# Receptance and key projections of the second block: three weight chunks as seven half-block products each

## The reference

```python
x = rmsnorm(x, final_norm_g)            # end of the first block
xx = _token_shift(x) - x
xr, xk = x + xx * mu[0], x + xx * mu[2]     # xw, xa, xg, xv likewise, with their own mu
r = xr @ w_r                            # 512 x 1024 by 1024 x 1024
k = xk @ w_k                            # the same size
w, a, g: small products xw @ w1, xa @ a1 (64 columns each), xg @ g1 (128 columns)
v = xv @ w_v
kk = k * k_k; its norm over each head of 64 features is taken here too
```

## Time and profile before

| | us |
|---|---|
| median of three runs | 2712.99 |
| lowest and highest run | 2707.52 and 2714.55 |
| profiled execution, its own time | 2716.39 |
| profiled execution, span of the trace | 2714.6 |
| this stage, from its first product to the start of the last `gemm` | 1081.34 to 1222.62 |

### The profile page before, as it was taken

The page is one execution under the profiler, slowest core; times in us unless marked ns, Lnnn a source line. Parts: engine busy times, 40 slices in busy tenths (PEclk is TensorE's granted clock), DMA queues, the critical chain, the costliest instruction groups (busy, mean ns, idle before and its releaser), DMA issues. The chain is left out here.

```text
span 2714.6 us, 46714 instructions
## 1 busy us (share of the span) xinstructions
PE 2584.1 (95%) x20608; PEld 1977.9 (73%) x20608; DVE 1243.7 (46%) x1965; ACT 515.3 (19%) x1032; POOL 548.9 (20%) x361
## 2 busy tenths in 40 slices
PE   6999889989999999999899999999999999999998
PEld 4555568854888887444788568888878764888886
DVE  2213235454899944222677454442242474545233
ACT  3222122321111101112455210000010261000001
POOL 0000055520000000000222023443333100443342
PEclk9999999999999999999999999999999999999999
DMA  7123100021212123111000021222222101122220
GB/s 300 71 116 155 63 2 3 3 94 62 93 67 89 66 85 128 47 62 63 34 4 4 2 93 67 89 93 93 90 83 93 63 1 62 63 93 93 77 78 32
DMA packets 17369, 195.32 MB, mean 72 GB/s; under 512 B 1896, under 2 KB 3048, under 8 KB 5392
## 3 DMA queue, kind: packets, MB, share of 16 engines
q1 hardware_dynamic: 17168, 192.34, 18.8%
HBM read 190.22 MB, written 2.12 MB: 71 GB/s over the span
## 5 line engine op out<-in xcount | busy, mean ns | idle before, releaser
L3322 PE MATMUL psum<-arena,weight_ring 128*128 128x256 f32 x3072 | 671.2, 379 | 2.9 <-ACT arena L3212 2.9
L3322 PEld LDWEIGHTS psum<-arena,weight_ring 128*128 128x128 f32 x3072 | 582.7, 190 | 86.0 <-ACT arena L3212 5.3
L1862 PE MATMUL psum<-arena,weight_ring 128*128 128x256 f32 x1584 | 348.2, 381 | 5.0 <-DVE arena L2038 4.0
L1862 PEld LDWEIGHTS psum<-arena,weight_ring 128*128 128x128 f32 x1584 | 301.6, 191 | 48.7 <-issue 6.4
L492 PE MATMUL psum<-arena,weight_ring 128*128 128x512 f32 (+1 forms) x672 | 250.5, 531 | 3.4 <-DMA weight_ring<-in_w_in 2.6
L492 PEld LDWEIGHTS psum<-arena,weight_ring 128*128 128x128 f32 x672 | 127.5, 193 | 118.5 <-issue 102.6
L2408 POOL TENSOR_TENSOR arena<-arena,consts_sb 128x512 f32<-128x512 f32 x9 | 11.4, 1271 | 726.8 <-ACT arena L2784 688.8
L3421 POOL TENSOR_TENSOR weight_ring<-arena,weight_ring 128x1024 f32<-128x1024 f32 x32 | 79.3, 2477 | 378.3 <-PE psum L3322 378.3
L229 PE MATMUL psum<-arena,weight_ring 128*128 128x512 f32 x320 | 137.8, 592 | 0.0
L3411 POOL TENSOR_TENSOR arena<-weight_ring 128x1024 f32<-128x1024 f32 x32 | 77.1, 2408 | 288.5 <-issue 172.7
L3444 ACT ACTIVATE arena<-psum 128x512 f32<-128x512 f32 (+1 forms) x24 | 12.6, 524 | 621.0 <-PE psum L3322 621.0
(11 more groups left out here) (482 smaller groups left out, 3688.8 us busy)
## 6 DMA issues: line engine op xcount, KB each, us to landing
weight_ring<-in_mlp_up SPq DMA_DIRECT2D x16, 2048.0 KB, 8.0
weight_ring<-in_mlp_down SPq DMA_DIRECT2D x16, 2048.0 KB, 8.0
weight_ring<-in_ada SPq DMA_DIRECT2D x12, 2048.0 KB, 11.4
weight_ring<-in_gate_up SPq DMA_DIRECT2D x11, 2048.0 KB, 7.8
weight_ring<-in_w_in SPq DMA_DIRECT2D x7, 2048.0 KB, 11.6
weight_ring<-in_w_o SPq DMA_DIRECT2D x4, 2048.0 KB, 7.9
weight_ring<-in_w_kv SPq DMA_DIRECT2D x4, 2048.0 KB, 8.0
weight_ring<-in_down_a SPq DMA_DIRECT2D x4, 1536.0 KB, 6.1
```

The source lines that it names most:

```text
L1862: mm = pe.matmul(g.banks[i][:, pair * half:(pair + 1) * half], left[:, j, pair * P:(pair + 1) * P], right(j), start=first and j == 0, stop ...
L3322: mm = pe.matmul(g.banks[i][:, pair * HALF:(pair + 1) * HALF], left[:, j, pair * P:(pair + 1) * P], right(j), start=first and j == 0, stop ...
```

## The change

Chunk 0 of `w_r` stays as it is. Chunks 1, 2 and 3 (the second of `w_r`, both of `w_k`) are multiplied by seven products of half blocks into banks 0 to 6. `key_sums` moves from bank 6 to bank 7 and to later places: its first half behind the two 64-column products, its second half behind the third small product. POOL gets a block of its own, with four weight sums a chunk; the first pair, `weight_sums(1)`, has nothing to wait for but the landed chunk. DVE gets `sides` (four input sums for each of two inputs) and `take` (seven additions a chunk); ACT gets one copy a chunk and loses twelve, and its squares move behind the last `take`. Five semaphores are added.

```diff
@@ -2168,10 +2168,27 @@
+    near, far = slice(0, HALF), slice(HALF, SEQ)
+    side = [view(g, V_AT + 1024 * n, 4, HALF) for n in range(4)]
+    s1 = view(g, 20480, 4, 256)
+    p1, u2, v_ = (view(g, 21504 + 512 * n, 2, HALF) for n in range(3))
...
-        s = stage_sems(g, ctx, "lora_in", "xx", "first", "mixed", "ksq", "kstat", "kroot", "kinv", *RMS_SEMS)
+        s = stage_sems(g, ctx, "lora_in", "xx", "first", "mixed", "ksq", "kstat", "kroot", "kinv", "w_sums", "side", "prod", "p1",
+                       "took", *RMS_SEMS)
...
+        def out_part(c, half, toks):
+            first = 4 * (c % 2) + 2 * half
+            return outs[c // 2][:, first:first + 2, (near, far)[toks]]
...
@@ -2187,7 +2204,7 @@
-                            mm = pe.matmul(g.banks[6][:, 8 * p + 2 * tile:8 * p + 2 * tile + 2],
+                            mm = pe.matmul(g.banks[7][:, 8 * p + 2 * tile:8 * p + 2 * tile + 2],
...
@@ -2208,15 +2225,54 @@
+                def product(c, i, left, right):
+                    if c == 1:
+                        if i != 1:
+                            pe.wait_ge(g.acc_free, group0 + 4)
+                    elif i == 0:
+                        pe.wait_ge(s.p1, c - 1)
+                    elif i == 6:
+                        pe.wait_ge(g.acc_free, group0 + 4 * c)
+                    else:
+                        pe.wait_ge(s.took, 6 * (c - 2) + (0, 1, 3, 5, 2, 6)[i])
+                    for pair in (0, 1):
+                        cols = slice(pair * P, (pair + 1) * P)
+                        for j in range(4):
+                            mm = pe.matmul(g.banks[i][:, pair * HALF:(pair + 1) * HALF], left[:, j, cols], right[:, j, :],
+                                           start=j == 0, stop=j == 3)
+                    if i < 6:
+                        mm.then_inc(s.prod, 1)
+                    else:
+                        mm.then_inc(g.acc_ready, 4)
...
                 rms_pe(g, pe, s, norm)
                 first_receptances()
-                group = group0 + 4
-                for j in range(2):
-                    pe.wait_ge(s.mixed, KD * (j + 1))
-                    for i in (0, 1) if j else (1,):
-                        group = gemm(g, pe, chunk0 + 2 * j + i, group, KD, 512,
-                                     [(0, lambda k: mixed[j % 2][:, k, :], SEQ)])
-                key_sums(0)
+                for c in (1, 2, 3):
+                    source = mixed[c // 2]
+                    sides = 4 * (c // 2)
+                    a11, a12, a21, a22 = quads(c)
+                    landed(pe, c)
+                    pe.wait_ge(s.mixed, KD * (c // 2 + 1))
+                    if c == 1:
+                        product(c, 1, a12, source[:, 4:8, near])
+                        product(c, 0, a11, source[:, 0:4, near])
+                    else:
+                        product(c, 0, a11, source[:, 0:4, near])
+                        product(c, 1, a12, source[:, 4:8, near])
+                    pe.wait_ge(s.w_sums, 4 * c - 3)
+                    pe.wait_ge(s.side, sides + 1)
+                    product(c, 2, s1, side[0])
+                    pe.wait_ge(s.w_sums, 4 * c - 2)
+                    pe.wait_ge(s.side, sides + 2)
+                    product(c, 3, a21, side[2])
+                    pe.wait_ge(s.w_sums, 4 * c - 1)
+                    pe.wait_ge(s.side, sides + 3)
+                    product(c, 4, a11, side[1])
+                    pe.wait_ge(s.side, sides + 4)
+                    product(c, 5, a22, side[3])
+                    pe.wait_ge(s.w_sums, 4 * c)
+                    product(c, 6, a12, source[:, 4:8, far])
+                group = group0 + 16
                 w = chunk_at(g, pe, chunk0 + 4, KD, 256)
                 for j, (lo, hi, row) in enumerate(((0, 64, 0), (64, 128, 64), (128, 256, 0))):
                     pe.wait_ge(s.mixed, KD * (j + 3))
@@ -2228,28 +2284,49 @@
                     mm.then_inc(g.acc_ready, 1)
                     group += 1
                     if j == 1:
-                        key_sums(4)
+                        key_sums(0)
+                key_sums(4)
                 pe.wait_ge(s.mixed, KD * 6)
                 gemm(g, pe, chunk0 + 5, group, KD, 512, [(0, lambda k: values[k], SEQ)])
...
+            @block.gpsimd
+            def _(pool):
+                def weight_sums(c):
+                    a11, a12, a21, a22 = quads(c)
+                    landed(pool, c)
+                    if c >= 2:
+                        pool.wait_ge(s.prod, 6 * (c - 2) + 3)
+                    pool.tensor_tensor(s1, a21, a22, ALU.add).then_inc(s.w_sums, 1)
+                    pool.wait_ge(s.w_sums, 4 * c - 3)
+                    pool.tensor_tensor(a21, a11, a21, ALU.subtract).then_inc(s.w_sums, 1)
+
+                def second_sum(c):
+                    a11, a12, a21, a22 = quads(c)
+                    pool.wait_ge(s.w_sums, 4 * c - 2)
+                    pool.wait_ge(s.prod, 6 * (c - 1) + 2)
+                    pool.tensor_tensor(a11, s1, a11, ALU.subtract).then_inc(s.w_sums, 1)
+
+                def fourth_sum(c):
+                    a11, a12, a21, a22 = quads(c)
+                    pool.wait_ge(s.w_sums, 4 * c - 1)
+                    pool.tensor_tensor(a12, a12, a11, ALU.subtract).then_inc(s.w_sums, 1)
+
+                weight_sums(1)
+                for c in (1, 2, 3):
+                    second_sum(c)
+                    fourth_sum(c)
+                    if c < 3:
+                        weight_sums(c + 1)
...
+                def lora_out(i):
...
-                        act.activation(kn, g.banks[6][:, 0:64], ACT.Sqrt).then_inc(s.kroot, 1)
+                        act.activation(kn, g.banks[7][:, 0:64], ACT.Sqrt).then_inc(s.kroot, 1)
+                    if i >= 19:
                         ins = act.activation(outs[2][:, i - 19, :], bank[:, :], ACT.Copy)
                     elif i == 16:
                         ins = act.activation(wa[0:64, :], bank[0:64, :], ACT.Tanh)
...
-                    if 8 <= i < 16:
-                        act.wait_ge(g.acc_free, group0 + i + 1)
-                        if i == 15:
-                            act.wait_ge(s.kstat, 1)
-                        act.activation(ksq[:, (i - 8) % 7, :], outs[1][:, i - 8, :], ACT.Square,
-                                       scale=g.v.k_k[:, i - 8:i - 7]).then_inc(s.ksq, 1)
+
...
+                for i in range(4):
+                    act.wait_ge(g.acc_ready, group0 + i + 1)
+                    act.activation(outs[0][:, i, :], g.banks[2 * ((group0 + i) % 3)][:, :], ACT.Copy).then_inc(g.acc_free, 1)
+                for c in (1, 2, 3):
+                    act.wait_ge(s.prod, 6 * (c - 1) + (2 if c == 1 else 1))
+                    if c >= 2:
+                        act.wait_ge(s.took, 6 * (c - 2) + 2)
+                    act.activation(p1.rearrange("p a n -> p (a n)"), g.banks[0][:, :], ACT.Copy).then_inc(s.p1, 1)
+                act.wait_ge(g.acc_free, group0 + 16)
+                for p in range(KD):
+                    if p == 7:
+                        act.wait_ge(s.kstat, 1)
+                    act.activation(ksq[:, p % 7, :], outs[1][:, p, :], ACT.Square, scale=g.v.k_k[:, p:p + 1]).then_inc(s.ksq, 1)
+                    if p < 2:
+                        lora_out(16 + p)
+                for i in range(18, 23):
+                    lora_out(i)
                 act.wait_ge(g.acc_free, group0 + 23)
 
...
+                def sides(j):
+                    source = mixed[j]
+                    x11, x12, x21, x22 = source[:, 0:4, near], source[:, 0:4, far], source[:, 4:8, near], source[:, 4:8, far]
+                    dve.wait_ge(s.mixed, KD * (j + 1))
+                    if j == 1:
+                        dve.wait_ge(g.acc_ready, group0 + 8)
+                    dve.tensor_tensor(side[0], x12, x11, ALU.subtract).then_inc(s.side, 1)
+                    dve.tensor_tensor(side[2], x22, x12, ALU.subtract).then_inc(s.side, 1)
+                    dve.wait_ge(s.side, 4 * j + 1)
+                    dve.tensor_tensor(side[1], x22, side[0], ALU.subtract).then_inc(s.side, 1)
+                    dve.wait_ge(s.side, 4 * j + 3)
+                    dve.tensor_tensor(side[3], x21, side[1], ALU.subtract).then_inc(s.side, 1)
+
+                def add(out, bank, other):
+                    both = g.banks[bank][:, :].rearrange("p (a n) -> p a n", a=2)
+                    return dve.tensor_tensor(out, both, other, ALU.add)
+
+                def take(c):
+                    done, took = 6 * (c - 1), 6 * (c - 1)
+                    if c >= 2:
+                        dve.wait_ge(s.took, took)
+                        dve.wait_ge(g.acc_free, group0 + 4 * c)
+                    dve.wait_ge(s.p1, c)
+                    dve.wait_ge(s.prod, done + 2)
+                    add(out_part(c, 0, 0), 1, p1).then_inc(s.took, 1)
+                    dve.wait_ge(s.prod, done + 5)
+                    add(u2, 4, p1).then_inc(s.took, 1)
```

(38 more changed lines are left out.)

14 lines of the change are left out of this document (11 added, 3 removed).

## The result

The changed kernel takes 2697.52 us in the median of 4 runs (2695.71 to 2697.79) against 2712.32 beside it (4 runs, 2707.52 to 2714.55): a ratio of 0.9941 with a 95% interval of 0.9925 to 0.9957, so 14.8 us less, where 7.9 were forecast. The forecast of 2705.1 with its range of 2700.0 to 2710.5 is missed on the low side. The profiled execution took 2697.26 us; before, it was 2716.39.

A forecast was written before the change was run, and what follows sets the result against it. PE's own work was taken to bound the stage; -9.89 products, +1.05 seam, +0.9 start and 0 clock gave -7.9 us, so 2705.1 us from the median 2712.99, range 2700 to 2710.5.

The forecast's parts named there:

- Products: Chunks 1 to 3 of the changed stage: 72.52 us in place of 82.41, so 9.89 us removed.
- All the slacks: In those chunks POOL, DVE, ACT and transfers finish before PE needs them; the tightest POOL sum has 4.4 us.
- The seam: Behind chunk 3 PE's first small product waits for the last addition of `take(3)`: 1.05 us added.
- The start, the port: At the stage's start a POOL sum holds up DVE's line 2284 through the shared port: 0.9 us added.
- The clock, "0 net": Half clock behind the two `key_sums` still costs 5.1 us, as before, so nothing is gained or lost.
- or also at the start: Half of a rival: 3.4 us at half clock at the stage's start, +1.7 us; chance 0.20 with the other half.
- `mix(2)` beside POOL's sums: Rival: POOL's sums delay DVE's `mix(2)` by up to 9.6 us; slower only if `take(2)` is late; chance 0.04.
- -9.89 + 1.05 + 0.9 + 0 = -7.9 us: The changed stage's products, seam, start and clock summed, and taken as the whole kernel's gain.
- POOL's clears, costed at 0: Five more POOL clears at the stage's exit, 0.07 us each on POOL alone, add 0 to the kernel.

The follow-up runs named there:

- Experiment 4: Two edits, each alone, to the changed kernel: POOL's first weight sum waits for the eighth mix, 2692.96 us; key sums dealt out one at a time, 2692.67 us.
- before_place47: The kernel before with exactly 47 more TensorE instructions (already satisfied waits) ahead of the last chunk's products of the changed stage: 2704.82 us, ratio 0.9980.
- before_again: The kernel before, unchanged, run once more: 2713.13 us, ratio 0.9999.
- after_again: The changed kernel, unaltered, run once more: 2698.26 us, ratio 0.9949.
- place 128: The kernel before with 128 more TensorE instructions ahead of the last chunk of the changed stage (place: added instructions modulo 256): 2709.72 us, ratio 0.9997.

## Why the prediction was wrong, step by step

- **Products: right.** 72.52 us were forecast for the three chunks and 72.69 measured, with no idle note. All the slacks held.
- **The seam: right.** 1.05 forecast; 0.94 idle, released by the last addition.
- **The start, the port: right.** "1.6 us" for line 2284 was 1.54, and the wait ahead of the first product grew by 0.85 for 0.9 forecast.
- **The clock, "0 net": mis-sized by 1.7 us.** Behind the sums the half clock stayed at 10.2 us, but behind the wait of 2.27 us at the start stand 3.4 more. That was half of a rival ("or also at the start"), priced at +1.7 and given 0.20 together with its other half. Experiment 4 shows that it comes with the POOL sums and goes with them. With this term the sum is -7.9 + 1.7 = -6.2, and the stage gave -6.1.
- **`mix(2)` beside POOL's sums: the mechanism came, and the cover held**, as its rival said it would have to fail for a loss.
- **The step that failed** is the one that carried the sum of one stage over to the kernel: "-9.89 + 1.05 + 0.9 + 0 = -7.9 us". It holds no term for the stages behind the change but POOL's clears, costed at 0. So it put the unchanged mixing stage at nothing, and that stage gave as much as the changed one. The 303 instructions that the change adds were costed as PE time alone; that they move all that follows against the instruction packets was in no term and no rival. That is worth 5.4 us by before_place47's ratio (0.0020 x 2710.65; 2.4 to 8.4 by its interval). In the two profiled executions the stage gave 6.2: the stalls fell by 6.1, half clock cost 1.7 more, and 1.8 less is unexplained. The repeats, before_again and after_again, give 6.3: 4.1 of stalls, 1.7 of half clock and 0.5.
- **What stays open.** 6.1 and some 6 make 12, of 14.8 measured. That is inside the interval of the result (11.7 to 20.3) and of after_again (8.7 to 18.7), so nothing more need be explained; whether there is more isn't shown. In the profiles the stretch ahead of the change is shorter too: the changed stage begins at 1071.6 us in the mean of the six traces with the stage as before, at 1068.2 in that of the nine with it changed. Their half clock ahead of it, 31.8 and 23.1 us in the mean, would make 4.4 us, more than the 3.4 between them. Code there is the same, and the single values overlap; whether that is chance wasn't tried. Nor is it shown why, of two stalls in neighbouring packets, the second packet begins only 2.7 to 3.8 us after its boundary.

## What to carry to other kernels

An idle note "issue" on a busy TensorE, amid very short products, is a place to look at: count its instructions to there, and see whether the stalls stand one packet (here 256) apart. Where they do, any change that adds or removes instructions ahead can move the time of stages that it doesn't touch, by 5 to 9 us here in most cases and by nothing in one (place 128), so a change is compared at the same place (pad with unneeded waits). The pad itself, or a bulk load kept away from such a stretch, can be a gain: each gave the kernel before 5 to 7 us. And thin work like these 2-column sums is better dealt out among dense products than kept together: the same records cost 5.1 us less.

## What the runs showed of the hardware that was not expected

- TensorE's instructions came in packets of 256 and only about one ahead: where it used one up in 2.7 to 3.3 us it stalled, as the next packet starts 0.9 to 1.5 us after the boundary before (0.2 and 1.8 at the ends) and PE goes on 2.2 to 2.9 us later.
- Beside a 2 MB weight load in flight such a packet began 3.2 to 4.5 us after the boundary; the stall was 3.58 us in before, and was gone when the load was held back.
- Two waits in a row on TensorE's queue became one instruction: 94 waits made 47, and 54 made 27.
- Beside POOL sums, `scalar_tensor_tensor` with two large SBUF inputs is held up as the subtraction is, eight taking 13.81 us for 5.39, and the POOL sums stretch too, from 2.36 us to 2.60 (at 1136.07 above) and up to 2.83. The Trainium skill, "SBUF — State Buffer", section "Who interferes with whom", has the first; the trace agrees.
- Sums of 0.95 us, each alone between dense products, left the granted clock at 1.00; four in a row of 3.7 us were followed by half clock in every trace of the changed kernel that kept them together.
